# A hybrid SSD, Hyena and MoE layer on one core: the smallest token group packed 64+64 and interleaved with the largest, and the SSD step projection moved and turned round

## The reference

```python
dt = softplus(p[..., COL_DT:COL_HY].reshape(bsz, L, 2, 32) + dt_bias)   # SSD step sizes: 64 columns of w_in
a  = -exp(a_log)                                                       # decays; cumulative sums of dt * a are exponentiated
...
g_idx   = argmax(h @ w_rg + b_rg)                     # each token chooses ONE of 4 groups
e_idx   = top-2 of the 4 experts inside that group    # softmax over the two, times the group's probability
hid     = silu(h @ w_gate[e]) * (h @ w_up[e])         # (2048 -> 512), for 16 experts
out     = sum_e combine[:, e] * (hid @ w_down[e])     # (512 -> 2048)
```

## Time and profile before

| | us |
|---|---|
| median of 3 runs (2507.03 to 2510.42) | 2509.18 |
| the profiled execution, its own time | 2508.52 |
| its span | 2507.0 |
| PE busy in the span | 2302.5 (92%) |
| DVE busy | 1503.9 (60%) |
| ACT busy | 1024.6 (41%) |
| first projection of the x, B, C block | 132.09 |
| first instruction of the next block (ACT) | 390.19 |
| its group loop begins (ACT, L889) | 453.04 |
| first matmul of expert 0 | 1782.39 |
| last read of the experts' sums begins (DVE, L2325) | 2472.40 |

### The profile page before, as it was taken

One profiled execution on the slowest core, in us unless ns is written; L12 is line 12 of the kernel. 1 busy time (PEld: TensorE's weight loads), 2 busy tenths in 40 slices (PEclk: granted clock), 3 DMA queues, 4 the chain that ended last, 5 costly groups with the idle time before them and its releaser, 6 DMA issues. The chain is left out here.

```text
span 2507.0 us, 34389 instructions
## 1 busy us (share of the span) xinstructions
PE 2302.5 (92%) x12901; PEld 1871.4 (75%) x12901; DVE 1503.9 (60%) x1967; ACT 1024.6 (41%) x1273; POOL 105.0 (4%) x113
## 2 busy tenths in 40 slices
PE   5789997889899999999999999884999999999995
PEld 0278887545689997788888999774688888878783
DVE  1345562555565467777765444545555568989896
ACT  2433331111355433333333334332444457767773
POOL 1000000000000012020201000000000000000000
PEclk9899996899899999999999999995999999999997
DMA  9833330699757654433443566631566679989992
GB/s 364 318 110 92 95 92 25 239 349 363 238 169 235 182 143 145 121 122 106 140 119 104 159 183 181 249 99 23 178 191 193 188 248 360 382 316 389 356 355 115
DMA packets 285408, 503.60 MB, mean 201 GB/s; under 512 B 18757, under 2 KB 158576, under 8 KB 283494
## 3 DMA queue, kind: packets, MB, share of 16 engines
q1 hardware_dynamic: 280310, 481.54, 57.3%
q0 software_dynamic: 4976, 20.43, 2.4%
HBM read 499.78 MB, written 2.13 MB: 200 GB/s over the span
## 5 line engine op out<-in xcount | busy, mean ns | idle before, releaser
L189 DVE TENSOR_TENSOR w_lo<-raw,w_hi 128x1024 fp32r<-128x1024 f32 x720 | 881.5, 1237 | 600.8 <-ACT w_hi L185 568.2
L185 ACT ACTIVATE w_hi<-raw 128x1024 fp32r<-128x1024 f32 x720 | 761.0, 1060 | 787.5 <-PE bank L197 772.4
L195 PE MATMUL bank<-h_hi,w_hi 128*128 128x256 f32 (+1 forms) x1664 | 514.6, 309 | 29.1 <-DVE w_lo L189 29.1
L196 PE MATMUL bank<-h_lo,w_hi 128*128 128x256 f32 (+1 forms) x1664 | 507.9, 305 | 0.0
L197 PE MATMUL bank<-h_hi,w_lo 128*128 128x256 f32 (+1 forms) x1664 | 507.9, 305 | 0.0
L195 PEld LDWEIGHTS bank<-h_hi,w_hi 128*128 128x128 f32 x1664 | 321.4, 193 | 46.6 <-issue 29.5
L196 PEld LDWEIGHTS bank<-h_lo,w_hi 128*128 128x128 f32 x1664 | 321.3, 193 | 14.3 <-issue 1.9
L197 PEld LDWEIGHTS bank<-h_hi,w_lo 128*128 128x128 f32 x1664 | 320.8, 193 | 12.8
L195 PE MATMUL bank<-w_hi,ys_hi 128*128 128x512 f32 x384 | 154.2, 402 | 17.8 <-DVE p_tmp L1835 11.4
L263 PE MATMUL bank<-raw,cpad 128*32 128x512 f32 x768 | 145.7, 658 | 23.1 <-DMA raw<-in_ada_w 23.1
L195 PE MATMUL bank<-w_hi,lt_hi 128*128 128x512 f32 x384 | 153.8, 400 | 2.8 <-DVE w_lo L189 2.8
(11 more groups left out here) (360 smaller groups left out, 3034.7 us busy)
## 6 DMA issues: line engine op xcount, KB each, us to landing
raw<-in_w_in SPq DMA_DIRECT2D x240, 512.0 KB, 4.0
raw<-in_ada_w SPq DMA_DIRECT2D x192, 512.0 KB, 7.5
raw<-in_moe_w_gate SPq DMA_DIRECT2D x128, 512.0 KB, 5.5
raw<-in_moe_w_up SPq DMA_DIRECT2D x128, 512.0 KB, 5.7
raw<-in_moe_w_down SPq DMA_DIRECT2D x128, 512.0 KB, 5.6
raw<-in_w_ssd_out SPq DMA_DIRECT2D x32, 512.0 KB, 4.8
raw<-in_w_hy_out SPq DMA_DIRECT2D x32, 512.0 KB, 3.6
raw<-in_w_o SPq DMA_DIRECT2D x32, 512.0 KB, 3.8
```

The costliest lines, as they stand in the source:

```text
L185: act.activation(self.k.w_hi[:, j % HL, :], self.k.raw[:, j % RAW, :], ACT.Copy).then_inc(self.hi_ready, 1)
L189: dve.tensor_tensor(self.k.w_lo[:, j % HL, :], self.k.raw[:, j % RAW, :], self.k.w_hi[:, j % HL, :].bitcast(F32), ALU.subtract).then_inc(s ...
L195: pe.matmul(out, lhs[0], rhs[0], start=start, stop=False)
L196: pe.matmul(out, lhs[0], rhs[1], start=False, stop=False)
```

## The change

**SSD steps.** The 64 step columns become one stationary operand of 128 columns: their fp32r part in columns 0 to 63, their remainder in 64 to 127 (`wdt_s`). The 512 tokens, hi and then lo, stream past it: 32 matmuls of 512 columns instead of 192 of 64. Four fp32 matmuls with a 128x64 matrix of two identities (`halves`, made on GpSimd) add the two halves and turn the result to tokens. All of this, the softplus, the decay sums and the exponentials go into iteration 0 of the x, B, C block: `steps` after its slab 0 on PE, `step_tokens` after slab 1, `decay_sums` after slab 4, with `step_lows`, `step_copy`, `softplus` and `decay_rest` at fixed places on DVE and `step_highs`, `softplus` and `decay_exps` on ACT.

**MoE.** The group with fewest tokens gets a tile of 64 tokens, `lt`: their rounded values in columns 0 to 63 and the rest in 64 to 127, as the stationary operand. An expert of it needs two passes (`mm2`), 4 matmuls a slab. The halves are added by fp32 matmuls with `halves8`, 4 for the gate and 4 for the up product (`fold`). Its sum over experts is kept in SBUF (`lout`), added to after each half of down. For e below 8, even e are experts of the largest group and odd e of the smallest (`who`). The two middle groups are experts 8 to 15, as before. SP waits for the largest group's number alone before it loads; the rest of the choice comes later.

The core of the diff, shortened:

```diff
+                def steps():
+                    pe.wait_ge(s.dt_lo, 1)
+                    for kt in range(KT):
+                        pe.matmul(k.psum[5][:], wdt_s[:, kt, :], k.h_hi[:, :, kt, :], start=(kt == 0), stop=False)
+                        mm = pe.matmul(k.psum[5][:], wdt_s[:, kt, :], k.h_lo[:, :, kt, :], start=False,
+                                       stop=(kt == KT - 1))
+                    mm.then_inc(s.dt_mm, 1)
+                def step_tokens():
+                    pe.wait_ge(s.zeroed, 2)
+                    pe.wait_ge(s.dt_sb, 1)
+                    for t in range(4):
+                        mm = pe.matmul(k.psum[7][:, t * 64:(t + 1) * 64], dtx[:, t * P:(t + 1) * P], halves[:],
+                                       start=True, stop=True)
+                    mm.then_inc(s.dt_tok, 1)
...
-                    project(i, 0, not last)
+                    project(i, 0, not last, (steps, step_tokens) if first else ())
...
-                    project(i, 1, not last)
+                    project(i, 1, not last, (decay_sums,) if first else ())
...
+        def who(e):
+            return (e % 2, e // 2) if e < BOTH else (e // PER, e % PER)
...
+                def mm2(out, both, rhs, start, stop):
+                    pe.matmul(out, both, rhs[0], start=start, stop=False)
+                    return pe.matmul(out, both, rhs[1], start=False, stop=stop)
...
+                        if little(e):
+                            mm = mm2(k.psum[bank][:], lt[:, kt, :], w, kt == 0, kt == KT - 1)
+                            continue
...
+                def fold(bank, a):
+                    for ft in range(4):
+                        mm = pe.matmul(k.psum[bank][:, ft * SM:(ft + 1) * SM], sg[:, a, ft * P:(ft + 1) * P], halves8[:],
+                                       start=True, stop=True)
+                    return mm
...
+                    if little(e):
+                        for c in range(2):
+                            cols = lout[:, (2 * half + c) * 512:(2 * half + c + 1) * 512]
+                            if e > 1:
+                                ins = dve.tensor_tensor(cols, k.psum[4 + 2 * half + c][:], cols, ALU.add)
```

More of the change, by code:

```diff
@@ new lines, in step_tokens, with decay_sums, total @@
+                def step_tokens():
[5 more added lines that the diff above has]
+                    mm.then_inc(s.dt_tok, 1)
+                def decay_sums():
+                    pe.wait_ge(s.dts, 1)
+                    out = k.psum[6][:].rearrange("p (n d h) -> p n d h", n=8, d=2)
+                    a = adr[:].rearrange("p t (d h) -> p t d h", d=2)
+                    def total(n, d, *terms):
+                        for m, (table, t) in enumerate(terms):
+                            mm = pe.matmul(out[:, n, d, :], table, a[:, t, d, :], start=(m == 0), stop=(m == len(terms) - 1))
+                        return mm
+                    for c in range(TT):
+                        total(c, 0, (k.upper, c))
+                        total(c, 1, (k.lower, c))
+                        total(2 + c, 0, (k.below, c))
+                        total(2 + c, 1, (k.above, c))
+                        for d in range(2):
+                            total(6 + c, d, (k.ones, c))
+                    total(4, 0, (k.upper, 2))
+                    total(4, 1, (k.lower, 2), (k.ones, 3))
+                    total(5, 0, (k.upper, 3), (k.ones, 2))
+                    total(5, 1, (k.lower, 3))
+                    whole = k.psum[7][:, 256:320].rearrange("p (d h) -> p d h", d=2)
+                    for d, (first, second) in enumerate(((3, 2), (2, 3))):
+                        pe.matmul(whole[:, d, :], k.ones, a[:, first, d, :], start=True, stop=False)
+                        mm = pe.matmul(whole[:, d, :], k.ones, a[:, second, d, :], start=False, stop=True)
+                    mm.then_inc(s.sums, 1)
@@ L540, in project @@
+                def project(i, p, both, between=()):
                     pe.wait_ge(s.padded, i * 4 + 2 * p + 2)
@@ L571, in _ @@
                 body(0, first=True)
+                pe.wait_ge(s.exps, 1)
                 with pe.Fori(1, 5) as i:
@@ new lines, in decay_rest @@
+                def decay_rest():
+                    dve.wait_ge(s.sums, 1)
+                    own.own(dve, dve.tensor_copy(u4[:, 0, 0:64], k.psum[7][:, 256:320]))
+                    own.own(dve, dve.scalar_tensor_tensor(
+                        out=ex[:, 4:6, :], in0=k.psum[6][:, 256:384].rearrange("p (t n) -> p t n", t=2), scalar=-1.0,
+                        in1=u4[:, 0, 0:64].unsqueeze(1).to_broadcast([P, 2, 64]), op0=ALU.mult, op1=ALU.add))
+                    dve.tensor_scalar(ex[:, 4:6, :], ex[:, 4:6, :], 0.0, None, ALU.min).then_inc(s.rest, 1)
+                    dve.wait_ge(s.exps, 1)
+                    own.own(dve, dve.tensor_tensor(ex[:, 2:6, :], ex[:, 2:6, :], dtr[:], ALU.mult))
@@ L672, in body @@
                         conv(i - 1, 1, True)
+                    else:
+                        step_copy()
                     for j in range(4, 8):
                         st.split_lo(dve, i, 8, j)
+                        if first and j == 5:
+                            softplus()
                     if not first:
@@ L677, in body @@
                     conv(i, 0, not last)
+                    if first:
+                        decay_rest()
                 body(0, first=True)
@@ L767, in _ @@
             def _(pe):
[L768 to L802, removed]
                 with pe.Fori(0, GROUPS) as g:
@@ L2225, in _ @@
[L2225 to L2231 removed]
+                counts = k.psum[4][:, 8:12]
```

361 lines of the change are left out of this document (229 added, 132 removed).

## The result

The changed kernel takes 2467.27 us (median of 4 runs, 2466.63 to 2467.5) where the kernel before, run beside it, takes 2508.83. The ratio is 0.9838, interval 0.9825 to 0.985: faster by 1.6%. On the 2509.18 us of the table that is 2468.5. The forecast was 2453 (2441 to 2468): the direction is right, the gain of 41.6 us is 14 short of the 56 that the sum gave, and the end of the range is just missed. Five later runs of the same kernel gave 2462.99 (0.9815, 0.9802 to 0.9829), which lies inside the range: whether the range is missed depends on the execution. The stage that holds most of the shortfall came out longer than forecast in both.

The account below looks back on a forecast made before the run. The prediction took the MoE as bound by PE and the SSD head as PE, ACT and DVE working in turn; -50.5 SSD, -1.4 routing, -9 MoE and +5 clock made -56 us, so 2453 (2441 to 2468).

Parts of the forecast that it names:

- the sum: Whole kernel: SSD -50.5, routing -1.4, MoE -9 and clock +5 make -56 us, giving 2453.
- SSD, what goes: SSD head: with it gone, the group loop and everything behind move 63.7 us earlier.
- the term that the sum put at nothing: SSD group loop: its own length was forecast to change by 0 us.
- Iteration 0: x, B, C block: added matmuls cost 13.2 us (7.3 steps, 5.9 fp32 records), with no PE wait.
- Routing: Routing and gather: DVE work +1.7, gather -3.4, about +0.3 at the end; net -1.4 us.
- The forecast price of a record: Routing's gather: 64 records at about 0.33 us, a sixth less with 320 columns instead of 384.
- MoE: Experts: -43.5 matmuls, +5.5 folds, +29 waiting for splits, so -9 us; clock falls add +5.
- the 38: Experts: PE work saved if the splits kept up, -43.5 + 5.5 = -38 us.
- The first (the splits keep up better): Experts: adds and folds fall where PE waits anyway, or the lead is longer; 2433 to 2439; chance 0.12.
- The second (the alternation gives all back): Experts: slower splits and 8 to 12 clock falls put MoE near +6, total 2463; chance 0.22.
- The fourth (slower): Experts' alternating part: the clock, once fallen in a short run, doesn't recover; slower than before; chance 0.02.
- The third (the SSD head comes back elsewhere: SSD: moved work delays a split or the group loop starts slowly; half of the 50.5 there, 2478; chance 0.03.

Follow-up runs that it names:

- experiment 7: Changed kernel with matmuls whose result nobody reads put into TensorE's waits ahead of and inside the SSD group loop: 2453.77 us, ratio 0.9782.
- the filled loops: Changed kernel with unread matmuls in TensorE's waits, 2453.77 us; the same plus an exponential ahead of the loop and interleaved slab order, 2419.72 us.
- with the silu: Kernel before with a one-column silu on ACT behind its three exponentials, so each group begins with a table load: 2513.53 us, ratio 1.0022.
- Experiment 6: Changed kernel with gate, up and down slabs of two groups interleaved and work between slabs three slabs behind instead of four: 2432.7 us, ratio 0.9692.

## Why the prediction came out as it did

**What failed** is one step of "SSD, what goes": everything behind the head "moves by 63.7 us", the group loop beginning "on a TensorE that stood idle a few microseconds, before as after". The loop was moved as if it had a fixed length. It has not: the term that the sum put at nothing measured 10.5 us (6.5 in the later execution), for two reasons.

- *The table load.* The block's head had been three exponentials, and they left ACT with the table that the loop wants. With them gone the loop is entered behind a silu and begins each of its four rounds with a load of 1.28 us. ACT's order of the changed kernel shows this load; the prediction read only PE's and DVE's. Its price at the head is 1.3 us: PE's first matmul starts 2.33 us behind DVE's first copy (405.16), before 1.08 (454.94 and 453.86 in the earlier trace rows). In the loop it is 2.9 (185.3 against 182.4) where the waits are filled, and three times 0.48 of wait where they aren't. The Trainium skill (ScalarE: Activation LUTs, "What ACT_TABLE_LOAD costs") gives 1283 ns for the load and about 1380 ns more for draining the engine; the trace has 1.28 for the load and no such time beside it (405.42 to 406.70, and the copy begins at 406.72), and PE waits 0.5 longer.
- *The clock.* Less half of its half-clock time (the estimate above) the loop is 179.1 us before and 181.1 after; the rest of the difference, 8.5, is clock. That the clock costs the loop time is shown by experiment 7; the share is an estimate, for the filled loops, with no half-clock time to take off, are 182.4 and 185.3 and not 179 and 181. Either filling costs 3 to 4 us itself or a stretch costs less than half its length; no run here tells which. The prediction had written down that 1.38 us of idle time leave the clock alone. Over nine profiles with both waits unfilled that is true of half of them: 18 of 36 waits of 1.37 us have a stretch at or behind them, 8 of 9 of the 2.48 us ones, and all 18 of the 2.96 us ones. The kernel before was shown in an execution that was lucky in this loop (1 of 4 and 2 of 3), and the prediction read only the first of its four short waits. How many of them a given execution meets isn't predictable from these rows, and whether the changed kernel is inclined to more stays open: with its SSD part the loop had 20.2 to 30.2 us behind the head (six profiles), with that of before 10.2 and 17.1, and 20.5 with the silu. The short waits were followed by a stretch in 14 of 24 cases with the changed SSD part and in 4 of 12 with the other, too few to tell.

**Iteration 0**: right in each of its steps (no wait in PE, 7.25, 0.8, 4.8 us), and 2.1 us more in all: 1.7 for the stretch behind the decay sums, which the sum didn't have, and 0.4 at the block's start.

**Routing**: the added DVE work costs 1.9 (PE's wait of 5.79 is 7.73 now, forecast +1.7); the gather gains 2.2, not 3.4. The forecast price of a record is right. These are the gather before and then after, each with its half-clock part in the first row and its full-clock part in the second:

```profile
1754.14:1757.60 3.46, 3.46 (x6) 1.93 (x7) 0.33 (x2) 0.49 (x1) 0.00 (x0) 0.50 0.87 268
1757.60:1776.30 18.70, 18.70 (x60) 11.01 (x59) 11.08 (x36) 6.87 (x14) 0.00 (x0) 1.00 0.47 176
```

```profile
1718.88:1724.03 5.15, 5.15 (x10) 3.38 (x11) 1.96 (x11) 0.97 (x4) 0.00 (x0) 0.50 1.05 393
1724.03:1739.00 14.97, 14.79 (x56) 10.16 (x55) 9.29 (x41) 6.51 (x27) 0.00 (x0) 1.00 0.10 38
```

At full clock records of 384 columns start 0.32 us apart and those of 320 columns 0.27, a sixth less. But the changed gather begins with 5.1 us at half clock instead of 3.5, which costs 0.8, and it waits 0.18 for DVE once. Net -0.2 for -1.4.

**MoE**: the mechanism and the size were right, -4 forecast with the clock, -2.2 measured. Idle time went up by 23.6 us (forecast 29), and the half-clock stretches behind waits by 13.6 us, about 6.8 lost (forecast 5). Part of the supply's price isn't in the idle rows at all. In the run of 12 these are the first matmuls of three slabs in a row:

```profile
1890.55 0.50 PE L2097 MATMUL bank<-w_hi,lt 128*128 128x512 f32 x1
...
1891.69 0.50 PE L2097 MATMUL bank<-w_hi,lt 128*128 128x512 f32 x1
...
1892.82 0.50 PE L2097 MATMUL bank<-w_hi,lt 128*128 128x512 f32 x1
```

They are 1.13 us apart, DVE's pace and not PE's 0.91, with no idle time shown: each slab waits 0.2 us, less than the modelled end of the matmul ahead of it. Experiment 6 shows that the order of slabs and of the work between them, and no fixed price, was what kept 28 us of the 38 back. The prediction saw the long runs as the cause and still didn't ask what another order would give.

**The rivals.** The first (the splits keep up better) didn't come. The second (the alternation gives all back) is nearest in number, 2463, but by accident: it put the experts at +6 with 8 to 12 falls of the clock, and they came out at -2.2 with four. The fourth (slower) didn't come: behind the waits the clock rose again within 3.4 or 6.8 us. The third (the SSD head comes back elsewhere, "the group loop starts as slowly as it did") had the right place and a chance of 0.03; a fifth of the 50 came back there. The falls after short idle times that the Trainium skill describes (TensorE: Matmul & The Clock Gate, "A second HAM failure mode: psum-queue depth-cycling") were weighed for the experts and not for the loop that already showed them; the traces bear the rule out in both (18 of 18 waits of 2.96 us, three of four of 2.33). By the Trainium skill each matmul looks normal; here the 512-column ones inside such a stretch last 0.63 us instead of 0.39.

## What to carry to other kernels

A loop that is moved takes its neighbours' leavings with it: look at the order of every engine, ACT's table loads too, for what the removed code had set up. Where TensorE waits one to three microseconds over and over, treat the stage's length as uncertain by half of what it may spend at half clock. Filling the wait with matmuls that nobody reads, if a PSUM bank is free, took 8 to 12 us off the loop with 26 to 33 us at half clock, and only 2 to 6 off the one with 16 to 23; it pays where the stretches are many. When short and long pieces share a pipeline with few buffers, alternate the pieces, not the experts: the averages were right from the start, the runs of 8 and 12 were what cost.

## What the runs showed of the hardware

- Behind the short idle times the half-clock stretches came out 3.4 or 6.8 us long, in every loop and expert stage that was read; a 512-column matmul in one lasts 0.63 us instead of 0.39.
- Idle times of 1.37 us in the group loop had such a stretch at or behind them in 18 of 36 cases, those of 2.48 in 8 of 9, those of 2.96 in 18 of 18; with the waits filled none was left.
- The clock also fell with TensorE never idle, in or right behind 44 fp32 records of 32 columns (174.4 to 177.8 in the changed kernel), in all nine profiles that have them.
- Executions of one kernel spread by up to 12.5 us (SSD part alone), and the clock goes with it: 17 runs of the kernel before reach from 2502.11 to 2513.28, at mean granted clocks of 0.953 and 0.948.
